# Two of four weight sums of each seven-product unit: from GpSimd tensor operations to accumulating DMAs

## The chip, the cores and the metric

The kernel runs on one core of one Trainium2 chip. The metric is the device time of one execution in microseconds (us), lower is better.

## The reference, cut to what matters

A hybrid decoder layer over 256 tokens of width 2048: a mixer (projection, mLSTM and retention heads, output projection), then a SwiGLU feed-forward network with 5632 hidden columns. The change touches only the feed-forward part:

```python
h = rmsnorm(x, g_ffn_pre[l])
ff = (jax.nn.silu(h @ w_gate[l]) * (h @ w_up[l])) @ w_down[l]
x = x + rmsnorm(ff, g_ffn_post[l])
```

All arrays are float32, 256x2048 activations against 2048x5632 (gate, up) and 5632x2048 (down) weights.

## The kernel before, in words

**Split products.** A float32 product is made of three TensorE products: each operand is split into a rounded upper part (hi) and the remainder (lo), and hi*hi, hi*lo and lo*hi are summed in PSUM. Activations stand ready as hi and lo tiles (h2T, ffT). Weights come from HBM as float32 into the buffer `raw` (four chunks of 128x2048, 1 MB each), then ScalarE copies a piece into `w_hi` (line 980 or 991), VectorE subtracts it from raw into `w_lo` (line 1561 or 1564), and TensorE multiplies (line 1692). `w_hi` and `w_lo` have four slots (AHEAD = 4), so ScalarE may start piece m only when TensorE has finished piece m-4 (`sub_done`).

**Groups and units.** The feed-forward runs over groups of 512 hidden columns for gate and up together. Group 0 is made in the ordinary way, groups 1 to 10 by the loops that matter here; then come two halves of the down projection. In a group, the contraction is cut into units of two 128-row tiles. A unit of kind R is ordinary: two pieces of twelve matmuls each. A unit of kind S uses a seven-product (Strassen-like) scheme on a 2x2 block split: 21 matmuls in place of 24, in four pieces of 6, 3, 6 and 6 matmuls. A full group is `RRSRSRSR`, so its S units are n = 2, 4 and 6; the last group is `RRSRSRRR` (n = 2 and 4 only); each down half has five S units (`RRSRRSRRSRRSRRSRRRRRRR`). In all 27 + 2 + 10 = 39 S units. Each weight-column block is 128x512; an S unit's chunk holds b12, b22, b11 and b21.

**The four weight sums of an S unit.** The seven products need four combinations of the blocks, made in place in `raw`, one after another:

- T3, GpSimd, line 613: b12 = b22 - b12, as soon as the chunk has landed.
- T2, VectorE, line 1570: b11 = b12 + b11. VectorE issues it behind the `w_lo` of piece 0 and ahead of that of piece 1, and it waits for T3 (`t3_ready`).
- T1, GpSimd, line 617: b22 = b22 - b11, after T2 (`t2_ready`).
- T4, GpSimd, line 619: b21 = b21 - b11, when also the `w_lo` of piece 1, which reads b21, is finished (`lo_done`).

Piece 2 (columns b12 and b11) waits on ScalarE for T3 and T2, and piece 3 (b22 and b21) waits on ScalarE for T1 and T4 (`t14_ready`). Every engine's queue is in order: GpSimd's sums of one unit are followed by T3 of the next S unit, in the down projection with `token_sums` (five GpSimd operations, lines 637 to 645) between T3 and T1. TensorE takes the pieces strictly in order, so a late piece 3 is an idle TensorE.

**Loads.** SyncE issues two 512 KB loads per chunk (line 544) when the chunk's last `w_lo` is done; they are the DMA traffic beside which all of this runs.

Of the kernel before, what the change touches and what calls it, by code (L numbers as in the profile page):

```python
# [206 lines left out]
def hybrid_layer(nc, x, positions, g_mix_pre, w_in, conv_w, conv_b, b_igate, b_fgate, g_mlstm_head,  # L207
                 g_ret_head, w_out, g_mix_post, g_ffn_pre, w_gate, w_up, w_down, g_ffn_post,
                 inv_freq, out):
    with ExitStack() as ctx:  # L210
# [3 lines left out]
        def sem(name):  # L214
            return ctx.enter_context(nc.semaphore(name))
# [79 lines left out]
        def ff(t, i=0):  # L295

            return parts(i)[:, 2 * t + 1, :]
# [74 lines left out]
        s_ready = sem("s_ready")  # L372
        t3_ready = sem("t3_ready")
        t2_ready = sem("t2_ready")
        t14_ready = sem("t14_ready")
        p1_out = sem("p1_out")
        part_step = sem("part_step")
        part_done = sem("part_done")
# [193 lines left out]
        @block.gpsimd  # L572
        def _(pool):
            pool.memset(ident, 0.0).then_inc(zeroed, 1)
            pool.memset(sel[:], 0.0).then_inc(zeroed, 1)
            pool.iota(rel[:, 0:2 * P], [[1, 2 * P]], base=0, channel_multiplier=-1,
                      allow_small_or_imprecise_dtypes=True).then_inc(zeroed, 1)
            pool.iota(rel[:, 2 * P:3 * P], [[1, P]], base=0, channel_multiplier=-1,
                      allow_small_or_imprecise_dtypes=True).then_inc(zeroed, 1)
            pool.wait_ge(zeroed, 4)  # L580
            pool.affine_select(ident, ident, [[-1, P]], ALU.not_equal, 1.0, base=0,
                               channel_multiplier=1).then_inc(consts, 1)
            pool.affine_select(sel[:], sel[:], [[-1, HEADS], [0, P]], ALU.not_equal, 1.0, base=0,
                               channel_multiplier=1).then_inc(consts, 1)

            pool.memset(wg_both[:].bitcast(F32), 0.0).then_inc(consts, 1)
            for c in (0, 2):
                pool.affine_select(rel[:, c * P:(c + 1) * P], rel[:, c * P:(c + 1) * P], [[1, P]],
                                   ALU.is_ge, 1e9, base=0, channel_multiplier=-1).then_inc(consts, 1)
            pool.memset(pre[:, :, 0:CONV - 1], 0.0).then_inc(consts, 1)  # L590


            pool.memset(v_sb[:, :, 0:HEADS, HD:HD + 1], 1.0).then_inc(consts, 1)
            pool.memset(v_sb[:, :, HEADS:2 * HEADS, HD:HD + 1], 0.0).then_inc(consts, 1)
            pool.memset(floor[:, :, HEADS:2 * HEADS], 1.0).then_inc(consts, 1)

            for h in range(HEADS):
                pool.wait_ge(decay_ready, HEADS + h + 1)
                for c in (0, 2):
                    block_ = decay[:, h, c * P:(c + 1) * P]  # L600
                    ins = pool.affine_select(block_, block_, [[1, P]], ALU.is_ge, 0.0, base=0,
                                             channel_multiplier=-1)
                ins.then_inc(masked, 1)

            pool.wait_ge(probs_ready, 2 * HEADS)
            pool.dma_start(g_post1[:], g_mix_post[0:1, :].partition_broadcast(P)).then_inc(post_in, 16)

            def weight_sums(i, n, plan, between=None):

                q, made = chunk_of(i, n), sums_index(i, n)  # L610
                b12, b22, b11, b21 = (raw[:, q, 512 * c:512 * (c + 1)] for c in range(4))
                pool.wait_ge(raw_up[q], up_arrived(i, n))
                pool.tensor_tensor(b12, b22, b12, ALU.subtract).then_inc(t3_ready, 1)  # L613
                if between:
                    between()
                pool.wait_ge(t2_ready, made + 1)
                pool.tensor_tensor(b22, b22, b11, ALU.subtract).then_inc(t14_ready, 1)  # L617
                pool.wait_ge(lo_done, ff_base(i) + (plan.base[n] + 2))
                pool.tensor_tensor(b21, b21, b11, ALU.subtract).then_inc(t14_ready, 1)

            with pool.Fori(1, FF_GROUPS - 1) as i:
                for n in SEVEN:
                    weight_sums(i, n, FULL)
            for n in SEVEN[:2]:
                weight_sums(FF_GROUPS - 1, n, FINAL)

            pool.wait_ge(sub_done, DOWN_FIRST)
            pool.dma_start(g_post2[:], g_ffn_post[0:1, :].partition_broadcast(P)).then_inc(post_in, 16)

            def token_sums(d, n):  # L630

                a11, a21 = d_whole[:, 0, 0:P], d_whole[:, 0, P:SEQ]
                a12, a22 = d_whole[:, 1, 0:P], d_whole[:, 1, P:SEQ]
                if d:
                    pool.wait_ge(d_step, 5 * d)
                    pool.wait_ge(d_ready, d)
                pool.tensor_tensor(d_whole[:], ffT[:, 2 * n:2 * n + 2, 0:SEQ].bitcast(F32),
                                   ffT[:, 2 * n:2 * n + 2, SEQ:2 * SEQ].bitcast(F32), ALU.add).then_inc(d_step, 1)
                pool.wait_ge(d_step, 5 * d + 1)
                pool.tensor_tensor(d_sum[:, 0], a21, a22, ALU.add).then_inc(d_step, 1)  # L640
                pool.tensor_tensor(d_sum[:, 2], a11, a21, ALU.subtract).then_inc(d_step, 1)
                pool.wait_ge(d_step, 5 * d + 2)
                pool.tensor_tensor(d_sum[:, 1], d_sum[:, 0], a11, ALU.subtract).then_inc(d_step, 1)
                pool.wait_ge(d_step, 5 * d + 4)
                pool.tensor_tensor(d_sum[:, 3], a12, d_sum[:, 1], ALU.subtract).then_inc(d_step, 1)

            pool.wait_ge(ff_lo, 2 * FF_GROUPS - 2)
            for half in range(2):
                for c, n in enumerate(DOWN_SEVEN):
                    d = len(DOWN_SEVEN) * half + c  # L650
                    weight_sums(FF_GROUPS + half, n, DOWN, between=lambda: token_sums(d, n))
# [3 lines left out]
        def _(act):  # L655
# [314 lines left out]
            def unit_hi(i, odd, plan, m):  # L970

                n, piece = plan.pieces[m]
                q, slot, arrived = chunk_of(i, n), ff_slot(i, odd, m), up_arrived(i, n)
                act.wait_ge(sub_done, ff_base(i) + (m - 3))
                if plan.units[n] == "R":
                    if piece == 0:
                        act.wait_ge(raw_up[q], arrived)
                    else:
                        act.wait_ge(raw_full[q], arrived + 16 * (R_FF + 2))
                    act.activation(w_hi[:, slot, :], raw[:, q, SUB * piece:SUB * (piece + 1)],  # L980
                                   ACT.Copy).then_inc(hi_done, 1)
                    return
                if piece == 0:
                    act.wait_ge(raw_up[q], arrived)
                    act.wait_ge(raw_full[q], arrived + 16 * (R_FF + 2))
                elif piece == 2:
                    act.wait_ge(t3_ready, sums_index(i, n) + 1)
                    act.wait_ge(t2_ready, sums_index(i, n) + 1)
                elif piece == 3:
                    act.wait_ge(t14_ready, 2 * sums_index(i, n) + 2)  # L990
                act.activation(slot_blocks(w_hi, slot, piece), seven_blocks(piece, q),  # L991
                               ACT.Copy).then_inc(hi_done, 1)

# [75 lines left out]
        def _(dve):  # L1069
# [429 lines left out]
            def up_sums(i, plan, c0, subs=None):  # L1499

                dve.wait_ge(part_done, 2 * i)
                dve.wait_ge(sub_done, ff_base(i) + (subs or plan.subs - 1))
                for t in range(TT):
                    dve.tensor_tensor(ff(t, i), ff(t, i), bank[:, c0 + 2 + t, :], ALU.add).then_inc(up_sum, 1)

            def gate_sum_of(i, t, c0):

# [26 lines left out]
            def seven_sums(j):  # L1534
# [4 lines left out]
                a12, a22 = whole[:, 1, 0:P], whole[:, 1, P:SEQ]  # L1539
                link(dve.tensor_tensor(whole, h2T[:, k:k + 2, 0:SEQ].bitcast(F32),  # L1540
                                       h2T[:, k:k + 2, SEQ:2 * SEQ].bitcast(F32), ALU.add))
                link(dve.tensor_tensor(s_sum[:, j, 0], a21, a22, ALU.add))
                link(dve.tensor_tensor(s_sum[:, j, 1], s_sum[:, j, 0], a11, ALU.subtract))
                link(dve.tensor_tensor(s_sum[:, j, 2], a11, a21, ALU.subtract))
                dve.tensor_tensor(s_sum[:, j, 3], a12, s_sum[:, j, 1], ALU.subtract).then_inc(s_summed, 1)

# [8 lines left out]
            def unit_lo(i, odd, plan, m):  # L1555
# [10 lines left out]
                   .then_inc(lo_done, 1)  # L1566
                if piece == 0:
                    dve.wait_ge(lo_done, ff_base(i) + (m + 1))
                    dve.wait_ge(t3_ready, sums_index(i, n) + 1)
                    dve.tensor_tensor(raw[:, q, 1024:1536], raw[:, q, 0:512], raw[:, q, 1024:1536], ALU.add)\  # L1570
                       .then_inc(t2_ready, 1)

            def partial_sums(i, plan, s0):
# [2 lines left out]
                p7, p5, p6 = bank[:, s0, :], bank[:, s0 + 1, :], bank[:, s0 + 3, :]  # L1576
                dve.wait_ge(sub_done, ff_base(i) + plan.after_seven)
                dve.wait_ge(p1_out, i)
                dve.tensor_tensor(u4, p1, p6, ALU.add).then_inc(part_step, 1)
                dve.wait_ge(part_step, 2 * i - 1)  # L1580
                dve.tensor_tensor(u3, u4, p7, ALU.add).then_inc(part_step, 1)
                dve.wait_ge(part_step, 2 * i)
# [537 lines left out]
```

## Time and profile before

| what | value |
|---|---|
| median of 3 runs | 1213.93 us (1213.62 to 1214.06) |
| span of the profiled execution | 1211.7 us |
| TensorE busy in the span | 1197.0 us (99%) |
| VectorE, ScalarE, GpSimd busy | 928.4, 674.2, 269.1 us |
| DMA | 229.61 MB, mean 189 GB/s |
| one feed-forward group | 42.7 us |

The profiler gives the span from the first to the last recorded instruction. For the profiled execution no separate device time is shown; the median of the unprofiled runs is 2.2 us above its span. A term worked out from the trace is added to the median. Times of rows are microseconds from the start of the span.

### The profile page before, as it was taken

To read this page: it belongs to the slowest core of one execution; us is meant where nothing else is said; L and a number is where in the kernel's file an instruction comes from. 1 tells how busy PE (TensorE), PEld (TensorE's weight loads), DVE (VectorE), ACT (ScalarE), POOL (GpSimd) and SP (SyncE) were. 2 spreads that over 40 slices of the span, in tenths; PEclk is the share of its full clock that TensorE was granted. 3 is DMA by queue.
4 is the path that set the end of the run, shared out by engine and by line. 5 is a ranking of instruction groups with operands and counts; after the bars stand their busy time and mean duration, and the time that the engine had idled before them with its cause. 6 is when DMAs were issued, how large, how long until landed. Compare 5 with 4: busy or idle time off the path is not lost.

```text
span 1211.7 us, 16368 instructions
## 1 busy us (share of the span) xinstructions
PE 1197.0 (99%) x5782; PEld 1000.2 (83%) x5782; DVE 928.4 (77%) x1163; ACT 674.2 (56%) x892; POOL 269.1 (22%) x202
## 2 busy tenths in 40 slices
PE   8999999999999999999999999999999999999997
PEld 7888888888888888888888888888888878887885
DVE  6657877877776755777888888788888788769866
ACT  5654666474564745655555555555655555446543
POOL 2000100000000000004333323432333287227710
PEclk9999999999999999999999999999999999999999
DMA  8657867768686565454665556566555746755562
GB/s 314 209 150 159 204 157 156 175 142 213 159 198 190 192 205 180 169 188 160 208 209 201 189 184 224 173 208 208 190 184 188 253 161 205 243 183 167 187 226 70
DMA packets 122547, 229.61 MB, mean 189 GB/s; under 512 B 8064, under 2 KB 24704, under 8 KB 121984
## 3 DMA queue, kind: packets, MB, share of 16 engines
q1 hardware_dynamic: 122208, 226.85, 60.5%
q0 software_dynamic: 288, 2.10, 0.4%
q8 instruction: 30, 0.49, 0.2%
q14 instruction: 21, 0.17, 0.0%
HBM read 226.83 MB, written 2.10 MB: 189 GB/s over the span
## 4 chain that ended last, share of the span: by engine, by line
PE 96%; DVE 2%; DMA 1%; ACT 0%; issue 0%; SPq 0%; DVEq 0%
PE bank L1692 95%; PE bank L1980 1%; DMA resid<-in_x 1%; DVE w_lo L1564 0%; PE bank L1697 0%; PE bank L1896 0%; DVE ff_out L1629 0%; DVE w_lo L1082 0%; DVE h L1109 0%; DVE resid L1685 0%; ACT w_hi L991 0%; PE bank L1953 0%; DVE hT L1095 0%; ACT L658 0%; ACT bank L1032 0%
## 5 line engine op out<-in xcount | busy, mean ns | idle before, releaser
L1692 PE MATMUL bank<-w_hi,h2T 128*128 128x512 f32 x1126 | 359.2, 390 | 0.0
L1082 DVE TENSOR_TENSOR w_lo<-raw,w_hi 128x1024 fp32r<-128x1024 f32 x172 | 209.4, 1223 | 128.9 <-ACT w_hi L668 128.2
L668 ACT ACTIVATE w_hi<-raw 128x1024 fp32r<-128x1024 f32 x172 | 181.1, 1060 | 174.0 <-PE bank L1692 156.6
L1692 PE MATMUL bank<-hT,w_hi 128*128 128x512 f32 x768 | 271.7, 397 | 0.0
L1564 DVE TENSOR_TENSOR w_lo<-raw,w_hi 128x1024 fp32r<-128x1024 f32 (+1 forms) x156 | 207.1, 1333 | 69.4 <-ACT w_hi L991 69.0
L1692 PEld LDWEIGHTS bank<-w_hi,h2T 128*128 128x128 f32 x1126 | 211.4, 188 | 43.9
L1561 DVE TENSOR_TENSOR w_lo<-raw,w_hi 128x1024 fp32r<-128x1024 f32 x170 | 213.6, 1288 | 34.4 <-ACT w_hi L980 33.7
L991 ACT ACTIVATE w_hi<-raw 128x1024 fp32r<-128x1024 f32 (+1 forms) x156 | 148.8, 955 | 158.3 <-PE bank L1692 134.0
L980 ACT ACTIVATE w_hi<-raw 128x1024 fp32r<-128x1024 f32 x170 | 174.8, 1056 | 89.3 <-PE bank L1692 89.1
L1692 PE MATMUL bank<-hT,w_lo 128*128 128x256 f32 x768 | 214.6, 279 | 0.0
L1692 PE MATMUL bank<-w_lo,h2T 128*128 128x512 f32 x543 | 211.3, 389 | 0.0
L1692 PE MATMUL bank<-w_hi,ffT 128*128 128x512 f32 x604 | 190.2, 390 | 0.0
L1692 PEld LDWEIGHTS bank<-hT,w_hi 128*128 128x128 f32 x768 | 144.0, 187 | 32.4
L1692 PEld LDWEIGHTS bank<-hT,w_lo 128*128 128x128 f32 x768 | 145.0, 189 | 0.0
L1692 PEld LDWEIGHTS bank<-w_hi,ffT 128*128 128x128 f32 x604 | 113.4, 188 | 25.3 <-DVE w_lo L1561 1.8
L1692 PEld LDWEIGHTS bank<-w_lo,h2T 128*128 128x128 f32 x543 | 102.0, 188 | 20.9
L617 POOL TENSOR_TENSOR raw<-raw 128x512 f32<-128x512 f32 x39 | 62.2, 1595 | 251.9 <-DVE raw L1570 251.9
L1692 PE MATMUL bank<-w_lo,ffT 128*128 128x512 f32 x302 | 117.6, 389 | 0.0
L613 POOL TENSOR_TENSOR raw<-raw 128x512 f32<-128x512 f32 x39 | 66.2, 1698 | 224.5 <-DMA raw<-in_w_up 190.0
L1692 PE MATMUL bank<-w_hi,hT 128*128 128x512 f32 x256 | 81.3, 393 | 0.9 <-DVE w_lo L1082 0.9
L1692 PE MATMUL bank<-w_hi,mixT 128*128 128x512 f32 x256 | 80.2, 391 | 0.0
L1692 PEld LDWEIGHTS bank<-w_lo,ffT 128*128 128x128 f32 x302 | 56.7, 188 | 11.4
(237 smaller groups left out, 1310.7 us busy)
## 6 DMA issues: line engine op xcount, KB each, us to landing
raw<-in_w_in SPq DMA_DIRECT2D x63, 1024.0 KB, 9.9
raw<-in_w_down SPq DMA_DIRECT2D x88, 512.0 KB, 4.9
raw<-in_w_up SPq DMA_DIRECT2D x80, 512.0 KB, 4.0
raw<-in_w_gate SPq DMA_DIRECT2D x80, 512.0 KB, 4.9
raw<-in_w_out SPq DMA_DIRECT2D x16, 1024.0 KB, 5.1
raw<-in_w_gate SPq DMA_DIRECT2D x4, 1024.0 KB, 5.3
raw<-in_w_up SPq DMA_DIRECT2D x4, 1024.0 KB, 6.0
resid<-in_x SPq DMA_DIRECT2D x2, 1024.0 KB, 7.2
```

What stands on the lines that cost most here:

```text
L613: pool.tensor_tensor(b12, b22, b12, ALU.subtract).then_inc(t3_ready, 1)
L617: pool.tensor_tensor(b22, b22, b11, ALU.subtract).then_inc(t14_ready, 1)
L668: act.activation(part_of(w_hi, rnd, s), src, ACT.Copy).then_inc(hi_done, 1)
L980: act.activation(w_hi[:, slot, :], raw[:, q, SUB * piece:SUB * (piece + 1)], ACT.Copy).then_inc(hi_done, 1)
L991: act.activation(slot_blocks(w_hi, slot, piece), seven_blocks(piece, q), ACT.Copy).then_inc(hi_done, 1)
L1082: dve.tensor_tensor(part_of(w_lo, rnd, s), raw_sub(rnd, s)[1], part_of(w_hi, rnd, s).bitcast(F32), ALU.subtract).then_inc(lo_done, 1)
L1561: dve.tensor_tensor(w_lo[:, slot, :], raw[:, q, SUB * piece:SUB * (piece + 1)], w_hi[:, slot, :].bitcast(F32), ALU.subtract).then_inc(lo_d ...
L1564: dve.tensor_tensor(slot_blocks(w_lo, slot, piece), seven_blocks(piece, q), slot_blocks(w_hi, slot, piece).bitcast(F32), ALU.subtract)\
L1692: return pe.matmul(out_, lhsT, rhs, start=start, stop=stop, skip_group_check=True)
L1980: ins = pe.transpose(bank[:, b0 + j // 2, c:c + P], ff(t)[:, j * P:(j + 1) * P], ident)
```

## The change

T3 and T4 become DMAs that GpSimd issues and that add the source block to the destination in SBUF. [...] The sums of the activations and three VectorE additions of partial results carry the matching signs, with as many operations as before. GpSimd's order changes: T4 is issued first, behind both waits (`lo_done` of piece 1 and `t2_ready`), and T1 comes behind it. `t14_ready` is split into `t1_ready` and `t4_ready`; a DMA counts 16. ScalarE's piece 2 no longer waits for T3 itself, only for T2, which waits for it. The loop over groups on GpSimd is written out by Python in place of a hardware loop.

```diff
                 pool.wait_ge(raw_up[q], up_arrived(i, n))
-                pool.tensor_tensor(b12, b22, b12, ALU.subtract).then_inc(t3_ready, 1)
+                pool.dma_start(b12, b22, accum_op=ALU.add).then_inc(t3_ready, 16)
                 if between:
                     between()
+                pool.wait_ge(lo_done, ff_base(i) + (plan.base[n] + 2))
                 pool.wait_ge(t2_ready, made + 1)
-                pool.tensor_tensor(b22, b22, b11, ALU.subtract).then_inc(t14_ready, 1)
-                pool.wait_ge(lo_done, ff_base(i) + (plan.base[n] + 2))
-                pool.tensor_tensor(b21, b21, b11, ALU.subtract).then_inc(t14_ready, 1)
-
-            with pool.Fori(1, FF_GROUPS - 1) as i:
+                pool.dma_start(b21, b11, accum_op=ALU.add).then_inc(t4_ready, 16)
+                pool.tensor_tensor(b22, b11, b22, ALU.subtract).then_inc(t1_ready, 1)
+
+            for i in range(1, FF_GROUPS - 1):
...
                 elif piece == 2:
-                    act.wait_ge(t3_ready, sums_index(i, n) + 1)
                     act.wait_ge(t2_ready, sums_index(i, n) + 1)
                 elif piece == 3:
-                    act.wait_ge(t14_ready, 2 * sums_index(i, n) + 2)
+                    act.wait_ge(t1_ready, sums_index(i, n) + 1)
+                    act.wait_ge(t4_ready, 16 * sums_index(i, n) + 16)
...
-                    dve.wait_ge(t3_ready, sums_index(i, n) + 1)
+                    dve.wait_ge(t3_ready, 16 * sums_index(i, n) + 16)
...
-                link(dve.tensor_tensor(s_sum[:, j, 0], a21, a22, ALU.add))
-                link(dve.tensor_tensor(s_sum[:, j, 1], s_sum[:, j, 0], a11, ALU.subtract))
+                link(dve.tensor_tensor(s_sum[:, j, 0], a22, a21, ALU.subtract))
+                link(dve.tensor_tensor(s_sum[:, j, 1], s_sum[:, j, 0], a11, ALU.add))
...
-                dve.tensor_tensor(u4, p1, p6, ALU.add).then_inc(part_step, 1)
+                dve.tensor_tensor(u4, p1, p6, ALU.subtract).then_inc(part_step, 1)
```

`token_sums` (GpSimd) and `up_sums` (VectorE) change signs in the same way.

## Rows read from the trace of the kernel before

**Rows 1.** The page, busy time of each engine: us, share, instructions.

```profile
PE 1197.0 (99%) x5782; PEld 1000.2 (83%) x5782; DVE 928.4 (77%) x1163; ACT 674.2 (56%) x892; POOL 269.1 (22%) x202
```

**Rows 2.** Windows, one feed-forward group; last: clock, DMA share, GB/s.

```profile
675.00:718.00 43.00, 43.00 (x196) 35.36 (x195) 36.27 (x38) 24.23 (x27) 14.92 (x10) 1.00 0.58 198
```

**Rows 3.** Waits, whole span: total us, times, longest.

```profile
ACT w_hi L991 <- POOL raw L619: 23.0, 9, 2.6
...
PEld bank L1692 <- DVE w_lo L1564: 8.0, 17, 1.6
```

**Rows 4.** The weight-load queue's waits between 506 and 931 us.

```profile
PEld bank L1692 <- DVE w_lo L1564: 3.0, 9, 0.4
```

**Rows 5.** Groups of GpSimd instructions: busy us, mean ns; idle before.

```profile
L613 POOL TENSOR_TENSOR raw<-raw 128x512 f32<-128x512 f32 x39 | 66.2, 1698 | 224.5 <-DMA raw<-in_w_up 190.0 <-DMA raw<-in_w_down 34.5
L619 POOL TENSOR_TENSOR raw<-raw 128x512 f32<-128x512 f32 x39 | 63.2, 1622 | 5.0 <-DVE w_lo L1564 5.0
L617 POOL TENSOR_TENSOR raw<-raw 128x512 f32<-128x512 f32 x39 | 62.2, 1595 | 251.9 <-DVE raw L1570 251.9
```

**Rows 6.** Timeline of an S unit n = 4: start us, duration us.

```profile
634.90 1.29 POOL L613 TENSOR_TENSOR raw<-raw 128x512 f32<-128x512 f32 x1
...
641.94 0.69 DVE L1570 TENSOR_TENSOR raw<-raw 128x512 f32<-128x512 f32 x1
...
642.55 0.69 DVE L1564 TENSOR_TENSOR w_lo<-raw,w_hi 128x512 fp32r<-128x512 f32 x1
...
644.35 1.29 POOL L619 TENSOR_TENSOR raw<-raw 128x512 f32<-128x512 f32 x1
...
646.07 1.06 ACT L991 ACTIVATE w_hi<-raw 128x1024 fp32r<-128x1024 f32 x1 [1.61 <-PE bank L1692]
...
649.01 0.19 PEld L1692 LDWEIGHTS bank<-w_hi,s_hi 128*128 128x128 f32 x1
```

**Rows 7.** Timeline of the next S unit, n = 6.

```profile
645.59 2.29 POOL L613 TENSOR_TENSOR raw<-raw 128x512 f32<-128x512 f32 x1
...
652.40 0.69 DVE L1570 TENSOR_TENSOR raw<-raw 128x512 f32<-128x512 f32 x1
...
653.01 0.69 DVE L1564 TENSOR_TENSOR w_lo<-raw,w_hi 128x512 fp32r<-128x512 f32 x1
...
657.11 1.06 ACT L991 ACTIVATE w_hi<-raw 128x1024 fp32r<-128x1024 f32 x1 [2.53 <-POOL raw L619]
658.21 1.23 DVE L1564 TENSOR_TENSOR w_lo<-raw,w_hi 128x1024 fp32r<-128x1024 f32 x1 [2.27 <-ACT w_hi L991]
...
659.49 0.19 PEld L1692 LDWEIGHTS bank<-w_hi,s_third 128*128 128x128 f32 x1 [0.31 <-DVE w_lo L1564]
```

**Rows 8.** Timeline of an S unit n = 2: piece 1's w_lo, piece 3's first weight load.

```profile
631.85 0.68 DVE L1564 TENSOR_TENSOR w_lo<-raw,w_hi 128x512 fp32r<-128x512 f32 x1
...
638.76 0.19 PEld L1692 LDWEIGHTS bank<-w_hi,s_hi 128*128 128x128 f32 x1
```

**Rows 9.** Timeline of an S unit of the down projection.

```profile
1005.73 1.58 DVE L1564 TENSOR_TENSOR w_lo<-raw,w_hi 128x512 fp32r<-128x512 f32 x1 [0.34 <-ACT w_hi L991]
...
1013.69 0.19 PEld L1692 LDWEIGHTS bank<-w_hi,d_ops 128*128 128x128 f32 x1 [0.25 <-DVE w_lo L1564]
```

**Rows 10.** DMA issues by line: count, KB each, median us to landing.

```profile
raw<-in_w_up SPq DMA_DIRECT2D x80, 512.0 KB, 4.0
raw<-in_w_gate SPq DMA_DIRECT2D x80, 512.0 KB, 4.9
raw<-in_w_out SPq DMA_DIRECT2D x16, 1024.0 KB, 5.1
...
out<-resid SPq DMA_DIRECT2D x8, 256.0 KB, 2.5
...
g_post<-in_g_mix_post POOLq DMA_DIRECT2D x1, 1024.0 KB, 7.0
```

**Rows 11.** Timeline, GpSimd's issue of one of its two DMAs.

```profile
965.71 0.58 POOL L628 DMA_DIRECT2D g_post<-in_g_ffn_post  x1 [21.88 <-PE bank L1692]
```

More of the change, by code:

```diff
@@ L374, in hybrid_layer @@
         t2_ready = sem("t2_ready")
-        t14_ready = sem("t14_ready")
+        t1_ready = sem("t1_ready")
+        t4_ready = sem("t4_ready")
         p1_out = sem("p1_out")
@@ L639, in token_sums @@
                 pool.wait_ge(d_step, 5 * d + 1)
-                pool.tensor_tensor(d_sum[:, 0], a21, a22, ALU.add).then_inc(d_step, 1)
+                pool.tensor_tensor(d_sum[:, 0], a22, a21, ALU.subtract).then_inc(d_step, 1)
                 pool.tensor_tensor(d_sum[:, 2], a11, a21, ALU.subtract).then_inc(d_step, 1)
                 pool.wait_ge(d_step, 5 * d + 2)
-                pool.tensor_tensor(d_sum[:, 1], d_sum[:, 0], a11, ALU.subtract).then_inc(d_step, 1)
+                pool.tensor_tensor(d_sum[:, 1], d_sum[:, 0], a11, ALU.add).then_inc(d_step, 1)
                 pool.wait_ge(d_step, 5 * d + 4)
@@ L1503, in up_sums @@
                 for t in range(TT):
-                    dve.tensor_tensor(ff(t, i), ff(t, i), bank[:, c0 + 2 + t, :], ALU.add).then_inc(up_sum, 1)
+                    dve.tensor_tensor(ff(t, i), bank[:, c0 + 2 + t, :], ff(t, i), ALU.subtract).then_inc(up_sum, 1)
             def gate_sum_of(i, t, c0):
```

## The prediction, made before the changed kernel was timed

> **What bounds the kernel now.** I read the page first: TensorE is busy 99% of the span, GpSimd 22% [rows 1]. The reader is to see that GpSimd's time as such is worth nothing. The window of one feed-forward group says the same more sharply: TensorE busy for all of its 43.0 us at full granted clock, VectorE for 36.27, GpSimd for 14.92, DMA engines 0.58 of the time [rows 2]. So the change can gain only where TensorE waits, and can lose wherever it makes TensorE wait.
>
> The waits come next. TensorE's weight loads wait for the `w_lo` of S units 8.0 us in all [rows 3], 3.0 us of it in nine pauses in groups 1 to 9 [rows 4]. The timeline says which nine: the S unit n = 6, where ScalarE's piece 3 waits for GpSimd's T4 (the 23.0 us in nine waits of [rows 3]) and TensorE then pauses 0.31 us for that piece [rows 7]. The other S units of a group have no such pause, but not much to spare either. The remaining 5.0 us lie in the down projection and at its start; a typical pause there is 0.25 us [rows 9].
>
> **The budget of piece 3.** T4 can't start before the `w_lo` of piece 1 is done, and TensorE wants piece 3 a fixed time later. Between them lie T4, ScalarE's copy (1.06), VectorE's subtraction (1.23) and the gaps: from ScalarE's start at 657.11 to TensorE's weight load at 659.49 it is 2.38 us, taken as 2.4 [rows 7]. What is left is the time from that `w_lo`'s end until T4's landing that costs nothing:
>
> - n = 2: end 631.85 + 0.68 = 632.53, TensorE's load at 638.76, which did not wait: 6.23 - 2.4 = 3.83 us [rows 8].
> - n = 4: end 642.55 + 0.69 = 643.24, load at 649.01, less the 0.04 by which it is later than its predecessor's spacing: 5.73 - 2.4 = 3.33 us [rows 6].
> - n = 6: end 653.01 + 0.69 = 653.70, load due at 659.49 - 0.31 = 659.18: 5.48 - 2.4 = 3.08 us [rows 7].
> - down: load due at 1013.69 - 0.25 = 1013.44. The `w_lo` of piece 1 started at 1005.73 and took 1.58 beside GpSimd's T1 [rows 9], where it takes 0.69 without it [rows 6]. T1 now comes behind that `w_lo`, so I take its end as 1006.42: 7.02 - 2.4 = 4.62 us (3.73 if it stays at 1.58).
>
> **The change part by part.**
>
> Removed from GpSimd: 39 T3 and 39 T4, 66.2 + 63.2 = 129.4 us [rows 5]. Worth nothing by itself, since GpSimd is not on the path; the one part that is, T4 behind T1 in n = 6, gives back its 3.0 us [rows 4]. The 5.0 us of the down part I leave: its pauses come from VectorE operations that share time with `token_sums`, which stay.
>
> Added on GpSimd: 78 DMA issues at 0.58 us [rows 11], together 45 us, hidden in its idle time. For T1 the issue is in the way: T1 now ends at 0.05 + 0.58 + 1.67 (its mean is 1.6, [rows 5]) = 2.3 us behind the `w_lo` of piece 1, or 2.9 if it runs at the 2.29 that GpSimd's operations take beside VectorE's [rows 7]. Both are under the smallest budget of 3.08, so T1 costs nothing as long as an issue takes under 0.75 us.
>
> T3 as a DMA: it is issued behind T1 of the unit before, about 2.35 us after that unit's `w_lo` of piece 1. For n = 4 this is at 632.53 + 2.35 = 634.9, where T3 stands today [rows 6], and T2 runs at 641.94: 7.0 us. For n = 6 it is 643.24 + 2.35 = 645.6 against T2 at 652.40: 6.8 us [rows 6, 7]. For n = 2 and in the down projection it is 10 us or more. VectorE waits for T3 in front of T2, with the `w_lo` of pieces 1, 2 and 3 queued behind it, and TensorE waits for those; up to 6.8 us the transfer is covered, beyond it all of VectorE stands still. Cost: nothing.
>
> T4 as a DMA is the disputed cost. No row shows an accumulating transfer or one from SBUF to SBUF. It moves 256 KB and reads two blocks for the one it writes. Lower end: a 256 KB store issued by SyncE lands after 2.5 us [rows 10]. Upper end: GpSimd's 1 MB transfer landed after 7.0 us [rows 10]. Between them I build it from rows: 2.5 for 256 KB; the second read is worth half of what 512 KB more costs (5.1 - 4.0 = 1.1), so 0.55; GpSimd's path cost 7.0 - 5.1 = 1.9 more than SyncE's at 1 MB, part of which may be that transfer's own broadcast source. That gives 3.05 without the surcharge and 4.95 with all of it. Besides, the chunk loads keep the same DMA engines busy 0.58 of the time [rows 2]. I take 4.4 us, nearer the upper one. Against the budgets:
>
> - n = 2: 0.57 x 10 units = 5.7 us
> - n = 4: 1.07 x 10 = 10.7 us
> - n = 6: 1.32 x 9 = 11.9 us
> - down: 0 (under 4.62; 6.7 us if the budget is 3.73)
>
> Sum 28.3 of new pauses, less the 3.0 that go: +25.3 us. ScalarE's order is fixed, so ordinary pieces behind piece 3 come late as well, but they take it 1.06 and VectorE 1.23 us each against TensorE's 2.7 per piece; they catch up before the next S unit, and the pause repeats at each unit without growing.
>
> The Trainium skill (DMA: Bandwidth & Descriptors, "Anatomy of one DMA") gives for a DMA issued by GpSimd about 2.0 us plus bytes over 436 GB/s. Its estimate for 256 KB is 2.6 us, and 3.2 us if both reads count; by 2.6 no unit would pause. Its estimate for the 1 MB transfer would be 4.4 us, where the trace has 7.0 [rows 10], which is why I do not follow it. The same page ("Issuing engines are not separate DMA queues") says that transfers from all issuers share the same 16 engines.
>
> The weight loads get 6 more transfers per group, read twice. A pair of loads for one chunk (1 MB) lands about 5.4 us after its first issue (4.9 for the second [rows 10], issued half a microsecond later), so six half-sized transfers are some 6 us more of 43, DMA share 0.58 to about 0.72. Chunks land several microseconds ahead of use; cost nothing. The sign flips keep every operation count: nothing. The written-out loop: nothing.
>
> **The rivals.**
>
> 1. T4 lands inside the budgets (3.2 us or less). For it: the 2.5 us row, and that both ends of the transfer are in SBUF. Against it: GpSimd's surcharge and the shared engines. Break-even is where 10(L - 3.33) + 9(L - 3.08) = 3.0, that is L = 3.37 us. Below 3.08 it gives -3.0, and up to 2 us more if VectorE's operations have fewer collisions with GpSimd's: 1213.9 - 4 = 1210 us, faster. The skill's rule above would give this result.
> 2. Between them, L of 3.24 to 3.5: gains and pauses cancel, 1211.5 to 1216.3, same.
> 3. The transfer takes 7 us, as GpSimd's only measured one. T4: 10 x 3.17 + 10 x 3.67 + 9 x 3.92 + 10 x 2.38 = 127.5 less 3.0: 1338 us; and T3 starts to hold VectorE too. For it only that row, of four times the bytes.
> 4. GpSimd's issue is the late one: an accumulating transfer takes 1.5 us to issue rather than 0.58, so T1 ends 3.2 to 3.8 us behind the `w_lo`. At 3.8: n = 4 0.47 x 10, n = 6 0.72 x 9, less 3.0: +8.2, 1222 us, slower, even with a fast T4.
>
> **How the numbers follow.** All terms come from one profiled execution of 1211.7 us span; the median is 1213.9, 2.2 us more, and I add the difference to the median: 1213.9 + 25.3 = 1239 us. Chances: forecast (L from 3.5 to 5.8 us) 0.55, its own range 1216 to 1292; rival 1 0.20; rival 2 0.08; rival 3 and anything over 5.8 us 0.11; rival 4 0.06. Faster by over 0.2% (about what a measurement of this kernel can tell from no change) 0.20, within 0.2% 0.08, slower 0.72. The 80% range leaves out the slowest transfers and reaches down to rival 1: 1209 to 1292.
>
> **What the changed profile would show.** Right: T4's DMA lands 4 to 5 us after its issue; ScalarE's line 991 waits for a DMA into raw some 29 to 39 times; TensorE's weight load pauses at piece 3 for 0.6 us (n = 2), 1.1 (n = 4), 1.3 (n = 6, where 0.31 is there today), little in the down projection; a group takes about 45 to 46 us instead of 42.7; VectorE does not wait in front of T2. Wrong by size if the landing differs: each 0.1 us is 2.9 us of the result. Wrong in kind if VectorE waits for T3, if ScalarE waits for T1 rather than T4, if R pieces run out of loaded weights, or if TensorE's granted clock falls in the new pauses.

## The result, and the profile after

The changed kernel takes 1259.5 us (median of 4, 1256.1 to 1266.6) against 1213.8 us: ratio 1.0376, 95% interval 1.0355 to 1.0397, so 3.8% slower. The forecast was 1239 us and slower, the range 1209 to 1292.

The page of the changed kernel, busy time per engine:

```profile
PE 1206.8 (96%) x5782; PEld 1003.4 (80%) x5782; DVE 921.3 (73%) x1163; ACT 669.1 (53%) x892; POOL 191.9 (15%) x202
```

GpSimd has 77 us less work and the kernel is slower all the same; TensorE now has idle time (compare [rows 1]). The nine groups from the first n = 2 unit to the tenth show it best. Before, they took 384 us and TensorE was busy in all of them; after, they take 422 us (the second window below reaches 1 us further and holds four matmuls more), 46.8 us each. The last three numbers are granted clock, DMA share and GB/s:

```profile
547.00:931.00 384.00, 384.00 (x1725) 316.21 (x1724) 322.52 (x333) 218.01 (x243) 130.77 (x82) 1.00 0.58 196
...
547.00:970.00 423.00, 392.40 (x1729) 318.41 (x1728) 326.47 (x334) 215.59 (x245) 82.60 (x83) 0.99 0.72 213
```

The waits name the cause directly. After (columns as in [rows 3]):

```profile
ACT w_hi L992 <- DMA raw<-raw: 109.7, 35, 5.5
...
PEld bank L1693 <- DVE w_lo L1565: 48.1, 30, 3.3
```

ScalarE waits 35 times for an accumulating DMA, at piece 3 of an S unit, where it used to wait nine times for GpSimd, and TensorE's weight load behind it waits 48.1 us instead of 8.0. VectorE waited for T3 once, for 1.0 us (its line 1571):

```profile
DVE raw L1571 <- DMA raw<-raw: 1.0, 1, 1.0
```

One S unit n = 4 in the timeline of the changed kernel answers to [rows 6]. The reader is to follow it downwards: piece 1's `w_lo`, the issue of T4, ScalarE's piece 3, VectorE, TensorE's weight load.

```profile
651.93 0.68 DVE L1565 TENSOR_TENSOR w_lo<-raw,w_hi 128x512 fp32r<-128x512 f32 x1
...
652.92 0.85 POOL L619 DMA_DIRECT2D raw<-raw  x1 [8.14 <-DVE w_lo L1565]
653.48 1.60 POOL L620 TENSOR_TENSOR raw<-raw 128x512 f32<-128x512 f32 x1
...
658.25 1.06 ACT L992 ACTIVATE w_hi<-raw 128x1024 fp32r<-128x1024 f32 x1 [4.85 <-DMA raw<-raw]
...
659.34 1.23 DVE L1565 TENSOR_TENSOR w_lo<-raw,w_hi 128x1024 fp32r<-128x1024 f32 x1 [3.16 <-ACT w_hi L992]
...
660.62 0.19 PEld L1693 LDWEIGHTS bank<-w_hi,s_hi 128*128 128x128 f32 x1 [2.70 <-DVE w_lo L1565]
```

From the `w_lo`'s end (652.61) to ScalarE's start (658.25) it is 5.64 us; from there to the weight load 2.37, the 2.4 of the prediction. Of the 5.64, 0.31 pass before the issue record begins; in the units of the groups it is 0.30 us everywhere. T1 ends at 655.08, far ahead of the DMA.

Reading every S unit of the timeline in this way gives a table. "Late" is the mean time from the `w_lo`'s end to ScalarE's start in the units where ScalarE waited for the DMA; pauses are sums of TensorE's weight-load waits for a `w_lo` in the unit.

| units | budget (prediction) | late | pauses, us | pauses before | predicted |
|---|---|---|---|---|---|
| 10 of n = 2 | 3.83 | 4.00 (8 units) | 2.5 | 0 | 5.7 |
| 10 of n = 4 | 3.33 | 4.95 | 17.8 | 0 | 10.7 |
| 9 of n = 6 | 3.08 | 5.33 | 19.8 | 3.0 | 11.9 |
| 10 in down | 4.62 | 4.91 (8 units) | 9.1 | 6.5 | 0 |

The new pauses are 49.3 - 9.5 = 39.8 us; the two spans differ by 1254.4 - 1211.7 = 42.7 us. A weight load runs ahead of its matmul, so its wait is not quite what TensorE loses. The starts of the matmuls give that: they are 0.23 us apart in an undisturbed stretch. What the spacings beyond that add up to has grown by 42.6 us, nearly the whole difference. Of it 37.8 us are pauses (2.0 at n = 2, 16.3 at n = 4, 17.0 at n = 6, 2.5 in the down part), and 4.8 us are the clock.

In the kernel before, the granted clock was 1.00 in all nine groups and in the down projection. In the changed kernel it fell three times, for 3.4 us each, from the higher level (2.4 GHz) to the lower one (1.2 GHz), from 614.4, 952.3 and 1020.6 us. Each time TensorE had just come out of a pause, by 0.6 to 1.1 us, in which its matmuls had stood still for 1.9 to 2.3 us; other pauses as long had no such stretch behind them. The first of the three, as a window and as matmuls:

```profile
614.40:617.80 3.40, 3.40 (x10) 2.61 (x9) 3.25 (x5) 1.23 (x2) 0.00 (x0) 0.50 0.89 287
...
613.47 0.50 PE L1693 MATMUL bank<-w_hi,s_hi 128*128 128x512 f32 x1 [1.89 <-DVE w_lo L1565]
613.81 0.40 PE L1693 MATMUL bank<-w_lo,s_hi 128*128 128x512 f32 x1
...
615.88 0.63 PE L1693 MATMUL bank<-w_lo,h2T 128*128 128x512 f32 x1
```

The four timed executions of the changed kernel go by the same number: 1256.1 us at a mean granted clock of 0.994 (the one that was profiled), 1259.1 at 0.993, 1259.9 at 0.991 and 1266.6 at 0.988.

### The profile page after: what moved, and what is told of

Same layout as the page of the kernel before. It is cut to its first block, busy times and chain, and to the rows that moved or that the text cites. A ratio compares the mean times of both kernels' runs of the same rounds, so it can differ in the third digit from the quotient of the medians.

```text
span 1254.4 us, 16342 instructions
## 1 busy us (share of the span) xinstructions
PE 1206.8 (96%) x5782; PEld 1003.4 (80%) x5782; DVE 921.3 (73%) x1163; ACT 669.1 (53%) x892; POOL 191.9 (15%) x202
## 3 DMA queue, kind: packets, MB, share of 16 engines
q0 software_dynamic: 11520, 22.55, 9.7%
## 4 chain that ended last, share of the span: by engine, by line
PE 61%; DVE 15%; DMA 12%; issue 8%; ACT 3%; DVEq 0%; SPq 0%; ACTq 0%
PE bank L1693 61%; DMA raw<-raw 11%; DVE w_lo L1565 5%; DVE w_lo L1562 4%; ACT w_hi L992 3%; DVE part L1523 1%; DVE part L1510 1%; DMA resid<-in_x 1%; DVE part L1505 1%; DVE part L1582 0%; DVE part L1580 0%; DVE part L1585 0%; DVE raw L1571 0%; PE bank L1698 0%; PE bank L1897 0%
## 5 line engine op out<-in xcount | busy, mean ns | idle before, releaser
L1083 DVE TENSOR_TENSOR w_lo<-raw,w_hi 128x1024 fp32r<-128x1024 f32 x172 | 209.3, 1222 | 128.6 <-ACT w_hi L669 127.9
L1565 DVE TENSOR_TENSOR w_lo<-raw,w_hi 128x1024 fp32r<-128x1024 f32 (+1 forms) x156 | 211.6, 1358 | 114.8 <-ACT w_hi L992 114.5
L1562 DVE TENSOR_TENSOR w_lo<-raw,w_hi 128x1024 fp32r<-128x1024 f32 x170 | 208.2, 1257 | 34.1 <-ACT w_hi L981 33.8
L619 POOL DMA_DIRECT2D raw<-raw x39 | 33.2, 852 | 347.8 <-DVE w_lo L1565 344.8
L614 POOL DMA_DIRECT2D raw<-raw x39 | 42.2, 1082 | 253.1 <-DMA raw<-in_w_up 217.1
```

Source lines behind the costliest of these rows:

```text
L614: pool.dma_start(b12, b22, accum_op=ALU.add).then_inc(t3_ready, 16)
L619: pool.dma_start(b21, b11, accum_op=ALU.add).then_inc(t4_ready, 16)
L1083: dve.tensor_tensor(part_of(w_lo, rnd, s), raw_sub(rnd, s)[1], part_of(w_hi, rnd, s).bitcast(F32), ALU.subtract).then_inc(lo_done, 1)
L1562: dve.tensor_tensor(w_lo[:, slot, :], raw[:, q, SUB * piece:SUB * (piece + 1)], w_hi[:, slot, :].bitcast(F32), ALU.subtract).then_inc(lo_d ...
L1565: dve.tensor_tensor(slot_blocks(w_lo, slot, piece), seven_blocks(piece, q), slot_blocks(w_hi, slot, piece).bitcast(F32), ALU.subtract)\
```

## The experiments

Each run stood beside runs of the kernel before on the same chip; the ratio is against those.

**Flipped signs only.** All four sums stay tensor operations in the old order, with the changed signs, the split semaphore and the loop written out:

```diff
-                pool.dma_start(b12, b22, accum_op=ALU.add).then_inc(t3_ready, 16)
+                pool.tensor_tensor(b12, b22, b12, ALU.add).then_inc(t3_ready, 16)
...
-                pool.wait_ge(lo_done, ff_base(i) + (plan.base[n] + 2))
                 pool.wait_ge(t2_ready, made + 1)
-                pool.dma_start(b21, b11, accum_op=ALU.add).then_inc(t4_ready, 16)
                 pool.tensor_tensor(b22, b11, b22, ALU.subtract).then_inc(t1_ready, 1)
+                pool.wait_ge(lo_done, ff_base(i) + (plan.base[n] + 2))
+                pool.tensor_tensor(b21, b21, b11, ALU.add).then_inc(t4_ready, 16)
```

> The flipped signs, the split semaphore and the written-out loop, with all sums as GpSimd operations in the old order. All theories: 1213.8 us within 2. Another time would put part of the result on these edits.

Measured: 1215.0 us, ratio 1.0009 (0.9997 to 1.0021). The side edits cost nothing that can be told. (The order of T4 ahead of T1 is not in this kernel; it comes with T4's DMA.)

**T4 alone as a DMA** (first two lines of the diff above).

> Only T4 is an accumulating DMA, in the new order; T3 is a GpSimd addition. Theory: all of the loss, 1250 to 1262 us. If T3's DMA shares in it by occupying queue and engines just behind T4's (it is issued 1.8 us after T4), T4 lands sooner than 4.9 us here and the time is 5 to 15 us below that of the full change.

Measured: 1253.3 us, ratio 1.0311 (1.0281 to 1.0340). T4's DMA alone makes most of the loss. The unit table gives late times of 4.88 (n = 4) and 5.19 us (n = 6), near the full change's 4.95 and 5.33, and a few of its n = 2 units are earlier. The full change is another 6.2 us slower by the medians. Where those lie is not shown: the weight-load waits of the two profiled executions are alike (50 and 49 us).

**T3 alone as a DMA** (the rest of that diff).

> Only T3 is an accumulating DMA; T1 and T4 are GpSimd tensor operations in their old order. Theory (T4's landing against the budget of piece 3 is the whole loss): T3 has 6.8 us or more before VectorE wants it and lands in 4 to 5, so 1213.8 us within 3, with the nine pauses of 0.3 us at n = 6 still there. Rival (any accumulating transfer hurts, by holding VectorE at T2, by GpSimd's 1.1 us issue, or by slowing the weight loads): at least 10 us slower.

Measured: 1209.7 us, ratio 0.9965 (0.9950 to 0.9979): 0.35% faster than the kernel before, the fastest complete kernel of this study. Neither theory had said so. The nine pauses at n = 6 are gone, and the weight-load waits in the down part fell from 6.5 to 2.5 us; by the starts of the matmuls this is 1.5 and 2.1 us, the whole 3.6 us by which the two spans differ. The timeline of this kernel for such a unit, against [rows 7]:

```profile
653.35 1.67 POOL L618 TENSOR_TENSOR raw<-raw 128x512 f32<-128x512 f32 x1 [6.47 <-DVE raw L1571]
...
654.97 1.29 POOL L620 TENSOR_TENSOR raw<-raw 128x512 f32<-128x512 f32 x1
655.04 2.30 DVE L1565 TENSOR_TENSOR w_lo<-raw,w_hi 128x1024 fp32r<-128x1024 f32 x1 [1.18 <-ACT w_hi L992]
...
656.76 1.06 ACT L992 ACTIVATE w_hi<-raw 128x1024 fp32r<-128x1024 f32 x1 [1.75 <-PE bank L1693]
```

and the same two operations in the kernel before:

```profile
654.61 1.32 DVE L1564 TENSOR_TENSOR w_lo<-raw,w_hi 128x1024 fp32r<-128x1024 f32 x1 [0.92 <-ACT w_hi L991]
654.81 2.27 POOL L619 TENSOR_TENSOR raw<-raw 128x512 f32<-128x512 f32 x1
```

Whichever of T4 and VectorE's `w_lo` of piece 2 starts second takes 1 us longer (2.27 instead of 1.29; 2.30 instead of 1.22). Before, it was T4, and ScalarE waited for it; here VectorE comes 0.07 us later than T4 and pays, where it has the time. In the down part the same happens with the first operation of `token_sums`. In the unit of [rows 9] it started at 1011.25 beside VectorE's `w_lo` of piece 3 (1011.60), which took 2.04 us. Without T3 on GpSimd it starts at 1007.99 in the same unit, and that `w_lo` (1009.97) takes 1.32 us. The Trainium skill (SBUF — State Buffer, "Who interferes with whom") says that a VectorE instruction with two SBUF inputs contends with a GpSimd one that reads SBUF, and that issue order decides who blocks; by that rule, the trace agrees.

**No second DMA, T4 reported late.** In this kernel there is no accumulating DMA; three chained clears of spare memory stand between T4 and its signal:

```diff
+                pool.tensor_tensor(b21, b21, b11, ALU.add).then_inc(t4_step, 1)
+                for k in range(1, 4):
+                    pool.wait_ge(t4_step, 4 * made + k)
+                    pool.memset(spare_row[:], 0.0).then_inc(t4_step, 1)
+                pool.wait_ge(t4_step, 4 * made + 4)
+                pool.sem_inc(t4_ready, 16)
```

> No accumulating DMA at all: the sums are GpSimd operations in the old order, but T4 is reported late, behind three chained 128x64 clears of spare memory of about 0.6 us each. T4 is then reported some 4.2 us (n = 2, 4), 5.2 us (n = 6) and 4.0 us (down) after piece 1's w_lo. Theory (pure lateness of T4 against the budgets 3.83, 3.33, 3.08 and 3.73): 10 x 0.37 + 10 x 0.87 + 9 x 2.1 + 10 x 0.3 - 3 = +31 us, 1245 us, moved with the clears' true length by 3.9 us per 0.1 us. Rival (the loss comes from DMA traffic or descriptors that slow other engines): under 1220 us.

Measured: 1232.4 us, ratio 1.0141 (1.0116 to 1.0167). The clears took 0.15 us each, not the 0.6 that I had guessed from no row, so the time lies between my two theories' numbers and has to be worked out anew. An S unit n = 4 of this run:

```profile
651.78 2.26 POOL L622 TENSOR_TENSOR raw<-raw 128x512 f32<-128x512 f32 x1
654.11 0.57 POOL L625 MEMSET spare_row<- 128x64 f32 x3
...
654.76 1.06 ACT L999 ACTIVATE w_hi<-raw 128x1024 fp32r<-128x1024 f32 x1 [3.31 <-POOLq L627]
```

ScalarE started 4.09 us behind the `w_lo` of piece 1 at n = 4 (the median) and 4.10 at n = 6; n = 2 and the down part were in time but for one small pause. The budgets make of that 10 x 0.76 + 9 x 1.02 - 3.0 = +13.8 us; measured +18.9. A late signal with no DMA in it costs the same kind of pauses, so the pauses of the changed kernel need no other explanation than T4's lateness. About 2 us of the 5 that the budgets miss are GpSimd's T3, which here still stretches the `w_lo` of piece 3 at n = 4 (1.43 us instead of 1.23); the rest is not broken down.

**What makes the DMA late: its bytes, the addition, the loads.** Three kernels leave out part of the work to price these (two timed runs each): half of T4's columns, T4's addition, and one of the two tiles of each weight load.

```diff
-                pool.dma_start(b21, b11, accum_op=ALU.add).then_inc(t4_ready, 16)
+                pool.dma_start(b21[:, 0:256], b11[:, 0:256], accum_op=ALU.add).then_inc(t4_ready, 16)
```

> The full change, but T4's DMA adds only 256 of the 512 columns (the other half of that sum is left out). From w_lo's end to ScalarE's start the full one took 4.95 us at n = 4 and 5.33 at n = 6. If the bytes set it, each falls by 0.7 us or more and the time by 13 us or more, to 1246 or less. If a fixed part sets it, it falls by under 0.3 us and the time stays above 1253.

```diff
-                pool.dma_start(b21, b11, accum_op=ALU.add).then_inc(t4_ready, 16)
+                pool.dma_start(b21, b11).then_inc(t4_ready, 16)
```

> The full change, but T4's DMA is a plain copy of b11 over b21 (the addition is left out), still issued by GpSimd. If the second read of an accumulating transfer costs the 0.55 us that the prediction gave it, the landing is that much earlier and the time 10 us lower, about 1249. If accumulating costs nothing beside a copy, the time stays within 4 us of 1259.

```diff
-                    sp.dma_start(raw[:, q, SUB * half:SUB * (half + 1)].rearrange("p (k c) -> p k c", k=2),
-                                 rows(w, 2 * n, 2, col, 512)).then_inc(full[q], 16)
+                    sp.dma_start(raw[:, q, SUB * half:SUB * half + 512].rearrange("p (k c) -> p k c", k=1),
+                                 rows(w, 2 * n, 1, col, 512)).then_inc(full[q], 16)
```

> The full change, but each weight load of the feed-forward loops and the down projection brings one of its two 128-row tiles (the other keeps old data), so the load traffic is halved, with as many DMAs. If T4 is late because it shares the DMA engines with loads in flight, n = 4 and 6 land as n = 2 mostly does (3.6 us), the pauses shrink to about 0.3 and 0.5 us, and the time is 1222 us within 8. If the path's own latency sets it, the time stays above 1245.

| kernel | time, us | ratio (interval) | late n = 4, n = 6, us | issue to landing n = 2, 4, 6, us |
|---|---|---|---|---|
| full change | 1259.5 | 1.0376 (1.0355 to 1.0397) | 4.95, 5.33 | 3.30, 4.61, 4.99 |
| T4 half the bytes | 1239.6 | 1.0213 (1.0165 to 1.0262) | 4.11, 4.46 | 2.68, 3.77, 4.12 |
| T4 a plain copy | 1237.1 | 1.0193 (1.0113 to 1.0272) | 4.00, 4.57 | 2.33, 3.84, 4.21 |
| loads halved | 1225.5 | 1.0097 (1.0068 to 1.0127) | 3.64, 3.63 | 3.30, 3.30, 3.30 |

"Late" counts only the units where ScalarE waited for the DMA, 8 of 10 and 8 of 9 with the plain copy. The last column is from the start of the issue record to the landing, in every unit (the median at n = 2, where a few units stand out; means at n = 4 and 6). By it half the bytes are worth 0.84 and 0.87 us under load and 0.62 at n = 2; leaving out the addition is worth 0.78 at both places under load and 0.97 at n = 2. The copy also moves in fewer packets (9024 instead of 11520 in GpSimd's queue), so what I call the second read is all that the addition brings along.

The two expectations that named the bytes and the loads came true (under 1246, and 1222 within 8). That of the plain copy named 1249, and 1237 came: 0.78 us instead of 0.55, and more besides. The times fell by more than the landings explain: in the profiled execution of the plain copy the clock did not fall, and in that of half the bytes it fell once. Part of their gain over the full change is the clock, not T4.

Bytes, addition and loads all count. Which part of a load it is (its place in a queue, the engines, the memory) these runs don't separate. With halved loads the lateness is not only shorter but the same everywhere, 3.61 to 3.70 us in all 19 units n = 4 and 6 of that run, where the full change had 4.42 to 6.32. This unit n = 4 of the run with halved loads answers to the one above:

```profile
649.40 0.85 POOL L619 DMA_DIRECT2D raw<-raw  x1 [8.13 <-DVE w_lo L1565]
...
652.73 1.06 ACT L992 ACTIVATE w_hi<-raw 128x1024 fp32r<-128x1024 f32 x1 [2.87 <-DMA raw<-raw]
...
655.10 0.19 PEld L1693 LDWEIGHTS bank<-w_hi,s_hi 128*128 128x128 f32 x1 [0.73 <-DVE w_lo L1565]
```

From issue to use 3.33 us. The budget then leaves 0.3 and 0.55 us of pause for n = 4 and 6; measured 0.43 and 0.71.

**T1 instead of T4 as the second DMA.** It needs no `lo_done`:

```diff
-                pool.wait_ge(lo_done, ff_base(i) + (plan.base[n] + 2))
                 pool.wait_ge(t2_ready, made + 1)
-                pool.dma_start(b21, b11, accum_op=ALU.add).then_inc(t4_ready, 16)
-                pool.tensor_tensor(b22, b11, b22, ALU.subtract).then_inc(t1_ready, 1)
+                pool.dma_start(b22, b11, accum_op=ALU.add).then_inc(t4_ready, 16)
+                pool.wait_ge(lo_done, ff_base(i) + (plan.base[n] + 2))
+                pool.tensor_tensor(b21, b21, b11, ALU.add).then_inc(t1_ready, 1)
```

This kernel leaves out the subtraction that T1 needs (it adds), so its result is not the layer's; the operations are as many and as large.

> T3 as a DMA as in the change, T1 instead of T4 as the second one: it needs only T2, so it is issued about 0.6 us earlier, and T4 is a GpSimd addition (T1 has a flipped sign here: b22 + b11). Theory of the budget: the same latency, 0.6 us more of budget at 29 units: 4.43, 3.93 and 3.68, so pauses 1.0 at n = 4 and 1.65 at n = 6, 10 + 15 less 3: about 1236 us. Rival (the loss is per accumulating transfer, wherever it is issued): 1255 or more.

Measured (two timed runs): 1263.9 us, ratio 1.0413 (1.0383 to 1.0444). My expectation of 1236 failed, and the number of its rival came. The issue did come earlier, but the landing did not. SyncE's loads and the second DMA in a unit n = 4 of this run:

```profile
650.60 0.42 SPq L545 DMA_DIRECT2D raw<-in_w_gate  x1
652.25 0.85 POOL L618 DMA_DIRECT2D raw<-raw  x1 [7.65 <-DVE raw L1571]
...
658.38 1.06 ACT L992 ACTIVATE w_hi<-raw 128x1024 fp32r<-128x1024 f32 x1 [4.60 <-DMA raw<-raw]
```

and the last load of the same place in the full change:

```profile
650.67 0.42 SPq L545 DMA_DIRECT2D raw<-in_w_gate  x1
```

In both, ScalarE's piece 3 starts 7.6 to 7.8 us after the last of the four loads (2 MB) was issued, although GpSimd issued at 652.25 in one and at 652.92 in the other. All units say the same: from issue to landing 5.55 us at n = 4 and 5.82 at n = 6, where the full change has 4.61 and 4.99, so the 0.6 us were lost, and 0.3 more. (Of the 1263.9 us some 11 are the clock, which was at its lower level six times in the feed-forward part of this run.) That made a new theory: here the loads in flight set the landing, not the issue. Two more kernels test it. The first is the control, all sums as tensor operations with halved loads:

> Control for the halved loads: all sums as GpSimd operations in the old order (as the run with flipped signs only) and one of the two 128-row tiles of each weight load left out. Theory (TensorE-bound, loads hidden): halving them gives nothing by itself, 1212 to 1216 us, so that the 1225.5 us of the full change with halved loads is still 10 us or more of late T4. Rival (fewer loads speed the kernel as such): under 1208.

Measured: 1214.9 us, ratio 1.0011 (1.0000 to 1.0022). Halving the loads gives nothing by itself. The second is T1 as the DMA with halved loads, again without T1's subtraction (here the second tile of each load is the one that is brought):

> T1 in place of T4 as the second DMA, issued 0.6 us earlier, now with halved loads (one of the two tiles of each load left out; T1 with a flipped sign). With full loads the earlier issue bought nothing: it landed at 658.38 where T4's had landed at 658.25 in almost the same schedule. Theory (the landing there is set by the loads in flight, not by the issue): with halved loads the 0.6 us count, T1 lands about 3.7 us behind T2 against budgets of 3.9 at n = 4 and 3.7 at n = 6, pauses near nothing, 1210 to 1216 us. Rival (T1 as a DMA is slow for a reason of its own, or each accumulating DMA costs): 1225 us or more.

Measured: 1209.8 us, ratio 0.9975 (0.9960 to 0.9991). A unit n = 4 of this run:

```profile
643.10 0.85 POOL L618 DMA_DIRECT2D raw<-raw  x1 [8.09 <-DVE raw L1571]
...
646.52 1.06 ACT L992 ACTIVATE w_hi<-raw 128x1024 fp32r<-128x1024 f32 x1 [1.89 <-DMA raw<-raw]
```

At n = 4 and 6 ScalarE starts 3.0 to 3.3 us behind the `w_lo` of piece 1, and no S unit of the groups has a pause. With the loads out of the way the earlier issue is worth its 0.6 us, and the second accumulating DMA then costs nothing: the time equals that of T3's DMA alone. The rival, a price on each accumulating DMA wherever it is issued, is out.

## Why the prediction was right or wrong

**Right: what bounds, and where the loss falls.** TensorE bounds, GpSimd's freed time is worth nothing, and the loss is TensorE's pause in front of piece 3, once per S unit. T4's DMA alone (1.0311) and a late signal with no DMA (1.0141) show it. ScalarE's 35 waits for the DMA lie in the 29 to 39 of the prediction. The 2.4 us chain from ScalarE to TensorE was 2.37 in the changed kernel.

**Right: T3 is covered, and T1 behind the issue is.** VectorE waited for T3 once, 1.0 us, in the first down unit, where T3 was issued right behind GpSimd's 1 MB load of `g_post` (1004.15 and 1004.74 us) and took 7.3 us to land. Everywhere else T3 was there 3.3 us or more before T2. The issue took 0.85 us in the record, not 0.58, but T1's record begins 0.56 us after it begins, and T1 is not what ScalarE waits for. Rival 4 did not come.

**What the size was made of.** The kernel lost 45.7 us where 25.3 were forecast, 1.8 times as much. Of the 20 us that the sum lacks, the pauses are 12.5 (37.8 instead of 25.3) and the clock in the profiled execution is 4.8; the median lies another 3.4 above that execution, at lower granted clocks.

**Too small: the term for T4's landing.** I gave one number, 4.4 us, to all places and 28.3 us of pauses. Measured from the `w_lo`'s end it is 4.95 at n = 4 and 5.33 at n = 6, so 17.8 and 19.8 us of pauses instead of 10.7 and 11.9; at n = 2 it is mostly 3.6, so 2.5 instead of 5.7. What I named only as a reason to lean to the upper end, that chunk loads share the DMA engines, is a term of its own: 1.3 to 1.7 us at n = 4 and 6, whose T4 is issued 2.25 us behind the last of four loads (2 MB; 650.67 and 652.92). In the changed kernel n = 2 has one pair of loads in front of it, the last of them 3.6 us ahead (685.39, T4 at 688.98), and ScalarE starts 3.62 us after the `w_lo`. The window's mean share of 0.58 [rows 2] hides this; the places of SyncE's issues in the timeline would have shown it. With halved loads the places in the groups are equal, at 3.6.

**Luck: how 4.4 us was built.** The prediction reached it from 3.05 us and most of a surcharge of 1.9 us for GpSimd's path. No run shows such a surcharge at this size: a plain copy of 256 KB issued by GpSimd landed after 2.33 us at n = 2, sooner than SyncE's store of the row (2.5), and the accumulating one landed after 3.30 where no load was close. What made up the difference were two things that the sum did not have: the loads just in front (1.3 to 1.7 us), named there only as a reason to lean, and the 0.30 us between the `w_lo`'s end and the start of the issue, which it took as 0.05 for T1 and left out for T4. That one number was too high at n = 2 (by 3.2 us of pauses) also hid part of what it lacked at n = 4 and 6 (15.0 us).

**Too small: the second read.** I took 0.55 us from load rows. Leaving out the addition made T4 land 0.78 us earlier at n = 4 and at n = 6, under load, and 0.97 at n = 2.

**Too small: the budget's sharpness.** With a lateness of 3.64 the budgets leave 0.31 and 0.55 us, measured 0.43 and 0.71: they were 0.1 to 0.2 us too wide.

**Wrong: that the down projection pays nothing.** Its pauses rose from 6.5 to 9.1 us. The budget was right: piece 1's `w_lo` took 0.69 us there, and units with T4 late by 4.4 to 4.7 us had no pause above 0.2 (the first unit of each half apart, which pauses in the kernel before as well). But lateness spread from 4.4 to 6.3 us, 4.9 on average. The unit at 1150 us, with 6.3, makes 1.7 us of pause by itself, two others (4.9 and 5.2) 0.6 and 0.5. With halved loads the rise is gone (6.8 us).

**Missed: the clock.** The sum has no term for it; the prediction names a granted clock that falls in the new pauses as a sign that it is wrong in kind. It fell, for three stretches of 3.4 us, worth 4.8 us in the profiled execution. The pauses remain the main loss, but they have a second price that the prediction left at nothing.

**Missed: T3's DMA gains.** I took back only the 3.0 us of n = 6, and as an effect of taking T4 off GpSimd. In fact T3's DMA alone gives 4 us with T4 still on GpSimd, through the collisions with VectorE that it removes or shifts. The nine pauses at n = 6 were worth 1.5 us of that, not 3.0: in the kernel before the matmuls around one start 0.27 and 0.34 us apart instead of 0.23, while the weight load waits 0.31. The other 2.1 us lie in the down part, whose pauses the prediction left as they were because `token_sums` stays. It stays, but without T3 ahead of it it runs at another time.

**A small slip.** Rival 2's lower end, 3.24 us, gives 10 x 0 + 9 x 0.16 - 3.0 = -1.6, that is 1212.3 us; the 1211.5 given for it belongs to 3.15 us. Nothing else is worked out from it.

**The formula of the Trainium skill** (DMA: Bandwidth & Descriptors, "Anatomy of one DMA"): its estimates of 2.6 and, with both reads, 3.2 us stand against 3.30 us from issue to landing with halved loads. With full loads the kernel's own traffic makes it 4.6 (n = 4) and 5.0 (n = 6) on average, and that decides the sign: at 2.6, plus the 0.30 us before the issue, there would have been no pause.

## What to carry to other kernels

Moving work from an engine that was not the bottleneck to a DMA freed nothing here and put the DMA's latency against a deadline. So work out, for each consumer, the time from the last input's readiness to the moment the bound engine wants the result, and compare the transfer's landing with that. Where it was long (T3, 6.8 us), the DMA was free and took an operation out of VectorE's way; where it was 3 to 4 us (T4), it was not. Price the landing at its place in the timeline, behind the loads that are in flight just then, not by the mean share. Add a term for the clock when a change makes TensorE pause.

## What the runs showed of the hardware that I had not expected

- A DMA issued earlier behind the same burst of loads did not land earlier: issued at 652.25 or 652.92, ScalarE started at 658.38 or 658.25. With halved loads the same 0.6 us were gained in full.
- An accumulating 256 KB transfer within SBUF took 3.33 us from issue to use with halved loads, and up to 6.0 us beside full ones (issued at 570.22, used at 576.24). Far from loads (n = 2) it landed after 3.30 us, half of it after 2.68, a plain copy of the same size after 2.33.
- GpSimd's DMA issue began 0.30 us after what released it had ended (652.61 and 652.92); a tensor operation of the same engine in the same place (653.26 and 653.35 in the run with T3 alone as a DMA) began after 0.09.
- Of the 22 times that TensorE's matmuls stood still for over 0.4 us, three were followed by 3.4 us at a granted clock of 0.50; matmuls then took 0.63 us instead of 0.39.
- Of a GpSimd and a VectorE operation that both read SBUF, the one that started 0.07 or 0.20 us later took 1 us longer, and which one it was decided over a weight-load wait of 0.3 us per group.
- A GpSimd clear of 128x64 took 0.15 us, where I had expected 0.6.
